# 64 turns of the identity matrix in the opening's waits of TensorE

## The chip, the cores and the metric

The kernel runs on one NeuronCore of a Trainium2 chip. The metric is the device time of one execution in microseconds (us). Three timed runs of the kernel before gave 3094.46, 3094.46 and 3095.07 us, so the median is 3094.46 us.

## The reference, cut to what matters

The program computes two layers of a diffusion backbone on 512 latent tokens and 256 context tokens, 1024 channels wide. Only the start of the first layer matters here:

```python
mod = jnp.split((silu_c @ w_mod[l] + b_mod[l])[:, None, :], 6, axis=-1)
modc = jnp.split(silu_cc @ w_mod[l] + b_mod[l], 6, axis=-1)
u = modulate(rmsnorm(h, g_mix_pre[l]), mod[0], mod[1])      # x * (1 + scale) + shift
uc = modulate(rmsnorm(hc, g_mix_pre[l]), modc[0], modc[1])
y, y_ctx = token_mixers(u, uc, w_in[l], ...)                # begins with u @ w_in
```

The tokens are normalised, then scaled and shifted by vectors that come from two silu'd conditioning vectors times `w_mod`, a matrix that has to be read from memory; then the large product with `w_in` begins. After that come four kinds of token mixers, a gated merge and a feed-forward block, twice.

## The kernel before, in words

Each engine has its own instruction stream, written out by hand and joined by semaphores; nothing is reordered at run time. The weight products are made of three matmuls each (`w_hi`·`u_hi`, `w_hi`·`u_lo`, `w_lo`·`u_hi`): ScalarE (ACT) rounds a landed weight unit to `w_hi` (L1811, in the opening L2132) and VectorE (DVE) makes the rest `w_lo` (L2422, in the opening L2717). `chunk_product` and `half_product` (L1140, L1152) are the two lines where TensorE (PE) multiplies such a unit.

The opening (function `opening(g)` of the tensor block) runs in this order on PE. `turn_tokens(t)` turns each of six token tiles with 8 transposes against `ident` (L1002), two banks of PSUM at a time; ACT and DVE copy them out (L2118, L2702; `x_copied`). `turn_vectors(0)` turns the small vectors. `mod_product(at, half)` (L1030) multiplies the silu'd conditioning vectors by half of the modulation block `at`, four matmuls of 32 columns side by side, each of them two instructions in the trace; it waits for `mod_landed` of its 1 MB load. `first_roots` (L1017) spreads the inverse roots of the norm that GpSimd (POOL, L3381) makes. ACT copies a finished modulation row out (L2097, `row_copied`), `mod_columns(at)` (L1044) turns it into columns of bank 5, DVE adds the bias (L2685, L2691, `pair_made`), and ACT then scales and shifts one channel block k of the tokens (L2103), rounds it to `u_hi` (L2107), and DVE makes `u_lo` (L2697, `first_low`). `first_chunk(g, k)` multiplies that block by the first weight unit: 12 matmuls.

The loads go out from SyncE (SP, queue q1) in program order: the six token tiles, the modulation blocks 0, 4, 1, then the first `w_in` unit, then the blocks 5, 2, 6, 3, 7 (L928, two halves each), the second layer's vectors, two `w_in` units (L852), and 12 small loads that repeat one row to all 128 partitions: `sink`, `gbias` and four of `lam_in` for each layer (L936 to L939). Block `at` of `mod_product` uses load `MOD_LOADS[at]` of (0, 4, 1, 5, 2, 6, 3, 7), so blocks 0 and 1 use loads 0 and 4, block 2 load 1, block 3 load 5. After the opening, SP waits until a 3 MB store of the turned tokens (`h_scratch`, issued by ACT at L2144 after `row(7)`, on queue q10) has landed, and only then issues the loads for the background work: 1 MB blocks of `w_mod` (L835), which DVE multiplies and sums (L2737, L2739) into `part`, and which PE turns in `back_unit` (L1115, four transposes) after waiting for `back_summed`. On DVE this summing stands ahead of the L2422 that makes the next `w_lo`, that of the third weight unit. DVE's first instruction after the opening (L2657) needs all 12 small loads. SP's wait for the store:

```python
                            if phases[index - 1][0] in ("opening", "close"):
                                sp.wait_ge(h_stored, 16 * stored)
```

PSUM banks: the token turns use banks 0 to 3, the vectors bank 4, the modulation columns bank 5, the spread roots 6 and 7, and the first chunks banks 0 to 3. `MOD_BANK` = (0, 1, 4, 6, 7, 4, 6, 7).

Of the kernel before, what the change touches and what calls it, by code (L numbers as in the profile page):

```python
# [27 lines left out]
P = 128  # L28
D_MODEL, SEQ, CTX_LEN, DEPTH, GRID_W, ROPE_BASE = 1024, 512, 256, 2, 64, 10000.0
TOK = CTX_LEN + SEQ  # L30
NT = TOK // P
# [334 lines left out]
def build(nc, x, c, ctx_in, c_ctx, w_mod, b_mod, g_mix_pre, g_mix_post, g_ffn_pre, g_ffn_post, w_in, a_sink,  # L366
# [6 lines left out]
    with stack:  # L373
# [616 lines left out]
        def _(pe):  # L990
# [15 lines left out]
            def turn_vectors(ll):  # L1006

                pe.wait_ge(vectors_in[ll], 16 * 10)
                nc.tensor.transpose(ps[:, 4, 0:N_ROWS], vec_rows[0:N_ROWS, ll, :],
                                    ident[0:N_ROWS, 0:N_ROWS]).then_inc(vec_turned, 1)  # L1010

            def first_roots():

                pe.wait_ge(first_norm, 2)
                for t in range(NT):
                    at = t % 3 * P
                    last = nc.tensor.transpose(ps[:, 6 + t // 3, at:at + P], root[:, t:t + 1].to_broadcast([P, P]),  # L1017
                                               ident[:, :])
                last.then_inc(first_spread, 1)

            def mod_product(at, half):

                if half == 0 and at < 2:
                    pe.wait_ge(x_copied[at], NT - 1)
                if half == 0 and at in (3, 4):
                    pe.wait_ge(x_scaled, KD)
                pe.wait_ge(mod_landed[MOD_LOADS[at]], 16 * 2)
                for c in range(4):
                    k = 4 * half + c
                    last = nc.tensor.matmul(ps[32 * c:32 * c + 32, MOD_BANK[at], 0:256], silu_wide[:, k, :],  # L1030
                                            mod_ring[MOD_LOADS[at]][:, k * 256:(k + 1) * 256], start=half == 0,
                                            stop=half == 1)
                if half == 1:
                    last.then_inc(row_ready, 1)
# [13 lines left out]
            def first_chunk(g, k):  # L1048
# [4 lines left out]
                for j in range(g.nt):  # L1053
                    chunk_product(g, g.u0 % 2, g.t0 + j, j, k)

            def opening(g):

                pe.wait_ge(consts_made, 1)
                for t in range(NT):
                    turn_tokens(t)  # L1060
                    if t == 4:
                        turn_vectors(0)
                pe.wait_ge(scalars_in, 1)
                mod_product(0, 0)
                first_roots()
                mod_product(0, 1)
                mod_product(1, 0)
                mod_columns(0)
                mod_product(1, 1)
                mod_columns(1)  # L1070
                for at in (2, 3):
                    mod_product(at, 0)
                    mod_product(at, 1)
                mod_columns(2)
                mod_columns(3)
                first_chunk(g, 0)
                first_chunk(g, 1)
                for at in (4, 5):
                    mod_product(at, 0)
                    mod_product(at, 1)  # L1080
                first_chunk(g, 2)
                mod_columns(4)
                mod_columns(5)
                for at in (6, 7):
                    mod_product(at, 0)
                    mod_product(at, 1)
                first_chunk(g, 3)
                mod_columns(6)
                mod_columns(7)
                first_chunk(g, 4)  # L1090
                first_chunk(g, 5)
                turn_vectors(1)
                ph.end_products(True)
                first_chunk(g, 6)
                first_chunk(g, 7)
# [2342 lines left out]
```

## Time and profile before

| | us |
|---|---|
| three timed runs | 3094.46, 3094.46, 3095.07 |
| median | 3094.46 |
| the profiled execution | 3094.94 |
| its span, first to last instruction | 3093.2 |
| PE busy | 3018.7 (98% of the span) |
| DVE busy | 1702.3 (55%) |
| ACT busy | 1135.5 (37%) |
| mean granted TensorE clock | 0.995 |

The profiled execution lies 0.48 us above the median; 1.7 us of it lie outside the span. In a timeline a row stands for one instruction or for several equal ones in a row: start, duration of all, engine, line, operation, output and inputs, count, and in brackets how long the engine had been idle and what ended that. The rows of a matmul end later than the next begins, since its tail is counted; the distance of starts is the true pace.

### The profile page before, as it was taken

The page shows a single profiled execution, that of the slowest core. Times are in us where ns is not written, and L with a number is a line of the kernel's source. Part 1 is how long each engine was busy: PE and PEld are TensorE (multiplying, and loading weights), DVE is VectorE, ACT ScalarE, POOL GpSimd, SP SyncE. Part 2 cuts the span into 40 slices and gives each one's busy share as a digit, 9 for nine tenths or more (in the row PEclk, how much of TensorE's full clock was granted, in tenths as well). Part 3 has the DMA queues.
Part 4 walks back from the last instruction along what each step waited for, and adds up shares of the span by engine and source line. Part 5 has one row for each costly group of instructions (what it writes and reads, how often), then busy time and mean ns, then how long its engine had stood idle before and what let it go on. Part 6 is the DMA issues. An engine that isn't in the chain of part 4 may idle for free.

```text
span 3093.2 us, 44400 instructions
## 1 busy us (share of the span) xinstructions
PE 3018.7 (98%) x17548; PEld 2704.4 (87%) x17548; DVE 1702.3 (55%) x3077; ACT 1135.5 (37%) x1919; POOL 187.3 (6%) x153
## 2 busy tenths in 40 slices
PE   8999999999999999999999999999999999999999
PEld 7999978998898899999999997887877977888887
DVE  4844377333367866763362563547444688655334
ACT  5243254333313544222212442435333235532223
POOL 0011000200020000000000000100100210000000
PEclk8999999999999999999999999999999999999999
DMA  8412311310252024531431442241320621543333
GB/s 291 143 34 95 114 42 29 130 62 28 82 170 69 28 96 150 164 115 49 131 109 46 141 130 71 67 138 42 116 75 28 203 68 50 164 136 97 107 89 102
DMA packets 349295, 309.32 MB, mean 100 GB/s; under 512 B 40670, under 2 KB 321196, under 8 KB 347692
## 3 DMA queue, kind: packets, MB, share of 16 engines
q1 hardware_dynamic: 326926, 240.65, 26.1%
q10 hardware_dynamic: 22174, 65.99, 5.9%
q8 instruction: 133, 2.18, 0.3%
q14 instruction: 62, 0.51, 0.1%
HBM read 272.89 MB, written 33.29 MB: 99 GB/s over the span
## 4 chain that ended last, share of the span: by engine, by line
PE 50%; DVE 5%; ACT 1%; issue 1%; DMA 1%; POOL 0%; ACTq 0%; POOLq 0%; DVEq 0%
PE ps L1140 32%; PE ps L1516 5%; PE ps L1152 4%; PE ps L1552 2%; DVE space L2739 1%; PE ps L1594 1%; PE ps L1129 1%; PE ps L1580 1%; PE ps L1546 1%; DVE w_lo L2422 1%; PE ps L1612 1%; DMA space<-in_w_mod 1%; DVE mx L3008 0%; PE ps L1115 0%; PE ps L1766 0%
## 5 line engine op out<-in xcount | busy, mean ns | idle before, releaser
L1140 PE MATMUL ps<-u_hi,w_hi 128*128 128x384 f32 (+1 forms) x1784 | 522.3, 352 | 1.8 <-DVE w_lo L2422 0.7
L1140 PE MATMUL ps<-u_hi,w_lo 128*128 128x384 f32 (+1 forms) x1784 | 517.8, 349 | 0.0
L1140 PE MATMUL ps<-u_lo,w_hi 128*128 128x384 f32 (+1 forms) x1784 | 517.7, 349 | 0.0
L2422 DVE TENSOR_TENSOR w_lo<-w_raw,w_hi 128x2048 fp32r<-128x2048 f32 x129 | 298.3, 2312 | 311.9 <-ACT w_hi L1811 307.9
L1140 PEld LDWEIGHTS ps<-u_hi,w_hi 128*128 128x128 f32 x1784 | 324.3, 188 | 22.2 <-issue 2.7
L1140 PEld LDWEIGHTS ps<-u_hi,w_lo 128*128 128x128 f32 x1784 | 326.3, 188 | 18.6
L1140 PEld LDWEIGHTS ps<-u_lo,w_hi 128*128 128x128 f32 x1784 | 326.3, 188 | 17.9
L1811 ACT ACTIVATE w_hi<-w_raw 128x2048 fp32r<-128x2048 f32 x129 | 246.0, 1907 | 206.2 <-issue 64.6
L1516 PE MATMUL ps<-u_hi,w_hi 128*128 128x384 f32 (+1 forms) x816 | 304.3, 373 | 6.2 <-ACT space L2185 3.5
L1516 PE MATMUL ps<-u_hi,w_lo 128*128 128x384 f32 (+1 forms) x816 | 294.9, 361 | 0.2
L1516 PE MATMUL ps<-u_lo,w_hi 128*128 128x384 f32 (+1 forms) x816 | 293.6, 360 | 0.0
L2739 DVE SCALAR_TENSOR_TENSOR space<-space,silu_c 128x256 f32<-128x256 f32 x560 | 246.7, 482 | 10.1
L3008 DVE TENSOR_REDUCE mx<-ps 128x1 f32<-128x768 f32 (+3 forms) x200 | 156.3, 782 | 115.0 <-PE ps L1552 88.8
L1880 ACT ACTIVATE space<-ps 128x768 f32<-128x768 f32 (+3 forms) x78 | 57.4, 736 | 362.7 <-PE ps L1140 359.0
L1516 PEld LDWEIGHTS ps<-u_hi,w_hi 128*128 128x128 f32 x816 | 154.1, 189 | 23.3 <-ACT space L2185 7.3
L1516 PEld LDWEIGHTS ps<-u_hi,w_lo 128*128 128x128 f32 x816 | 153.8, 189 | 12.1 <-issue 2.1
L1516 PEld LDWEIGHTS ps<-u_lo,w_hi 128*128 128x128 f32 x816 | 154.3, 189 | 10.5 <-issue 1.3
L1850 ACT ACTIVATE hid_hi<-space 128x768 fp32r<-128x768 f32 (+2 forms) x44 | 32.6, 740 | 314.2 <-DVE space L2457 314.2
L2457 DVE TENSOR_TENSOR space<-space,ps 128x768 f32<-128x768 f32 (+1 forms) x44 | 36.1, 821 | 186.2 <-PE ps L1140 180.8
L2201 ACT ACTIVATE space<-ps,nmx 128x768 f32<-128x768 f32 (+3 forms) x160 | 119.4, 747 | 48.2 <-DVE nmx L3014 46.7
L1152 PE MATMUL ps<-u_hi,w_hi 128*128 128x384 f32 (+1 forms) x400 | 128.7, 322 | 5.9 <-DVE w_lo L2422 1.8
L1552 PE MATMUL ps<-space 64*128 64x256 f32 (+2 forms) x784 | 129.3, 447 | 4.9 <-ACT space L2201 4.9
(338 smaller groups left out, 5429.1 us busy)
## 6 DMA issues: line engine op xcount, KB each, us to landing
w_raw<-in_w_in SPq DMA_DIRECT2D x288, 256.0 KB, 3.8
w_raw<-in_w_gate_up SPq DMA_DIRECT2D x176, 256.0 KB, 4.0
space<-in_w_mod SPq DMA_DIRECT2D x40, 1024.0 KB, 5.3
w_raw<-in_w_down SPq DMA_DIRECT2D x114, 192.0 KB, 2.9
w_raw<-in_w_branch SPq DMA_DIRECT2D x64, 256.0 KB, 3.7
w_raw<-in_w_out SPq DMA_DIRECT2D x48, 256.0 KB, 3.7
m_scratch<-space ACTq DMA_DIRECT2D x3, 3072.0 KB, 10.0
space<-in_w_mod SPq DMA_DIRECT2D x16, 512.0 KB, 8.9
```

The lines of the kernel that those rows point to most:

```text
L1140: last = nc.tensor.matmul(ps[:, 2 * (t % 2) + b, 0:a1 - a0], wv[w][:, k, j * P:(j + 1) * P], xx[:, k, a0:a1], start=(k == 0 and w == 0 and ...
L1152: last = nc.tensor.matmul(ps[:, bank, at:at + cols.stop - cols.start], wv[w][:, k, j * P:(j + 1) * P], xx[:, k, cols], start=(k == 0 and w ...
L1516: last = nc.tensor.matmul(ps[:, bank, 0:cols.stop - cols.start], wv[w][:, k, j * P:(j + 1) * P], xx[:, k, cols], start=k == 0 and m == 0, ...
L1552: last = nc.tensor.matmul(ps[:, 2 * slot + at // 512, at % 512:at % 512 + b - a], lhs, rhs(a, b), start=not deep, stop=not here)
L1811: A(w_hi[slot][:, :], w_raw[slot][:, :], ACT.Copy).then_inc(w_hi_done, 1)
L1850: A(hid_hi[:, kk, toks(g.lat)], space[:, 30 + s:31 + s, toks(g.lat)], ACT.Copy).then_inc(hid_hi_done, 1)
L1880: A(tile_at(dst_tile(g, it, s, j), g.lat), acc_of(g, it, s, j, t), ACT.Copy if g.kind == "copy" else ACT.Sigmoid, scale=HD ** -0.5 if g.na ...
L2201: A(p_slot(kind, n.map)[:, 0:w], view, ACT.Exp, bias=nmx[:, n.map % 4:n.map % 4 + 1], scale=c_scale[:, t:t + 1] if kind == "c" else SCALE[ ...
L2422: V.tensor_tensor(w_lo[slot][:, :], w_raw[slot][:, :], w_hi[slot][:, :].bitcast(F32), ALU.subtract).then_inc(w_lo_done, 1)
L2457: V.tensor_tensor(tile_at(30 + s, g.lat), tile_at(30 + s, g.lat), acc(t % 2, g.lat), ALU.mult).then_inc(hid_ready, 1)
L2739: ins = V.scalar_tensor_tensor(part[:, sg], w, silu_c[:, k, sg:sg + 1], part[:, sg], ALU.mult, ALU.add)
L3008: own.did(V.reduce_max(mx[:, c4:c4 + 1], view, AX))
```

## The change

It adds a helper, `idle_turns(count, bank)`, and four calls of it in PE's opening. A turn is `nc.tensor.transpose` of `ident` against `ident` into one of four 128-column places of the named bank. Nothing reads what they write. 8 turns stand after the token turns, 12 between the first half product of block 0 and `first_roots`, 8 before `mod_columns(1)` and 36 between blocks 2 and 3. The last two calls write bank 2, and wait first until ACT has copied all the token turns. Everything else keeps its order.

```diff
+            def idle_turns(count, bank):
+
+                if bank == 2:
+                    pe.wait_ge(x_copied[0], NT)
+                for i in range(count):
+                    at = i % 4 * P
+                    nc.tensor.transpose(ps[:, bank, at:at + P], ident[:, :], ident[:, :])
+
             def opening(g):
 
                 pe.wait_ge(consts_made, 1)
@@
                     turn_tokens(t)
                     if t == 4:
                         turn_vectors(0)
+                idle_turns(8, 5)
                 pe.wait_ge(scalars_in, 1)
                 mod_product(0, 0)
+                idle_turns(12, 5)
                 first_roots()
                 mod_product(0, 1)
                 mod_product(1, 0)
                 mod_columns(0)
                 mod_product(1, 1)
+                idle_turns(8, 2)
                 mod_columns(1)
-                for at in (2, 3):
-                    mod_product(at, 0)
-                    mod_product(at, 1)
+                mod_product(2, 0)
+                mod_product(2, 1)
+                idle_turns(36, 2)
+                mod_product(3, 0)
+                mod_product(3, 1)
                 mod_columns(2)
                 mod_columns(3)
                 first_chunk(g, 0)
```

## Rows read from the trace of the kernel before

**Rows 1.** The page's part 1: busy time and share of the span of each engine.

```profile
PE 3018.7 (98%) x17548; PEld 2704.4 (87%) x17548; DVE 1702.3 (55%) x3077; ACT 1135.5 (37%) x1919; POOL 187.3 (6%) x153
```

**Rows 2.** Timeline of PE, opening: start, duration, line, count, idle before and releaser.

```profile
4.72 4.32 PE L1002 MATMUL ps<-ident,x_tok 128*128 128x128 f32 x24 [4.72 <-DMA x_tok<-in_ctx]
9.31 1.06 PE L1002 MATMUL ps<-ident,x_tok 128*128 128x128 f32 x8 [0.28 <-ACT space L2118]
...
14.92 0.64 PE L1030 MATMUL ps<-space 128*32 128x256 f32 x8 [1.49 <-DMA space<-in_w_mod]
17.41 0.95 PE L1017 MATMUL ps<-ident,root 128*128 128x128 f32 x6 [1.85 <-POOL root L3381]
18.30 1.93 PE L1030 MATMUL ps<-space 128*32 128x256 f32 x16
...
22.78 0.98 PE L1044 MATMUL ps<-picks,space 128*128 128x2 f32 x4 [0.59 <-ACT space L2097]
23.69 1.93 PE L1030 MATMUL ps<-space 128*32 128x256 f32 x16
29.13 1.93 PE L1030 MATMUL ps<-space 128*32 128x256 f32 x16 [3.50 <-DMA space<-in_w_mod]
30.99 1.87 PE L1044 MATMUL ps<-picks,space 128*128 128x2 f32 x8
32.72 0.99 PE L1140 MATMUL ps<-u_hi,w_hi 128*128 128x384 f32 x2
```

**Rows 3.** Stretches: window, length, busy (count) by engine, granted clock, DMA share, GB/s.

```profile
18.00:18.50 0.50, 0.50 (x7) 0.24 (x9) 0.10 (x1) 0.00 (x0) 0.00 (x0) 0.56 1.11 356
...
38.50:39.00 0.50, 0.50 (x5) 0.50 (x4) 0.20 (x1) 0.00 (x0) 0.00 (x0) 0.96 0.91 267
```

**Rows 4.** The same view, of the token turns (L1002) alone: PE, weight loads.

```profile
4.70:7.70 3.00, 2.98 (x14) 3.00 (x15) 1.00 1.03 399
```

**Rows 5.** Timeline of PE, the same kinds of work at full clock.

```profile
39.74 1.93 PE L1030 MATMUL ps<-space 128*32 128x256 f32 x32
41.60 0.61 PE L1140 MATMUL ps<-u_hi,w_hi 128*128 128x384 f32 x2
...
43.81 0.95 PE L1044 MATMUL ps<-picks,space 128*128 128x2 f32 x8
```

**Rows 6.** Timeline of DVE: the low parts of channel blocks 1 and 2.

```profile
33.60 0.96 DVE L2697 TENSOR_TENSOR u_lo<-first_x,u_hi 128x768 fp32r<-128x768 f32 x1 [0.27 <-ACT u_hi L2107]
35.67 0.96 DVE L2697 TENSOR_TENSOR u_lo<-first_x,u_hi 128x768 fp32r<-128x768 f32 x1 [1.11 <-ACT u_hi L2107]
```

**Rows 7.** One line's instructions: the last modulation load, and its issue to landing.

```profile
L928 SPq DMA_DIRECT2D space<-in_w_mod x1: 1888/1888/1888, 31.9 to 31.9; - x1
...
DMA to landing us min/median/max: 9.2/9.2/9.2
```

**Rows 8.** Timelines of ACT's and SP's queues: the 3 MB store, the first background loads.

```profile
46.70 0.37 ACTq L2144 DMA_DIRECT2D h_scratch<-space  x1
...
58.69 1.00 SPq L835 DMA_DIRECT2D space<-in_w_mod  x2
```

**Rows 9.** DMA queues in the stretch 46 to 50: packets, MB, share of 16 engines.

```profile
q1 hardware_dynamic: 898, 0.19, 22.2%
```

**Rows 10.** The same in 51 to 57.

```profile
q10 hardware_dynamic: 99, 2.43, 94.2%
q1 hardware_dynamic: 99, 0.01, 1.1%
```

**Rows 11.** Timelines of DVE and PE, from the background load to the third weight unit.

```profile
64.28 0.17 DVE L2657 TENSOR_SCALAR nsink<-sink 128x16 f32<-128x16 f32 x1 [5.44 <-DMA lam_in<-in_d_lam_k]
...
67.17 0.62 DVE L2737 TENSOR_SCALAR space<-space,silu_c 128x256 f32<-128x256 f32 x2 [1.68 <-DMA space<-in_w_mod]
67.83 6.38 DVE L2739 SCALAR_TENSOR_TENSOR space<-space,silu_c 128x256 f32<-128x256 f32 x14
74.35 2.29 DVE L2422 TENSOR_TENSOR w_lo<-w_raw,w_hi 128x2048 fp32r<-128x2048 f32 x1
...
76.33 0.60 PE L1115 MATMUL ps<-ident,space 128*128 128x128 f32 x4
76.70 0.62 PE L1140 MATMUL ps<-u_hi,w_hi 128*128 128x384 f32 x2
```

**Rows 12.** A later wait and the clock after it: waits of PE, stretches as above.

```profile
PE ps L1219 <- POOL root L3318: 2.3, 1, 2.3
...
1752.00:1755.40 3.40, 3.40 (x12) 3.40 (x11) 3.40 (x5) 0.00 (x0) 0.00 (x0) 0.50 0.42 117
```

## The prediction

> **What bounds the kernel.** I read the page's busy times first: PE is busy for 98% of the span, DVE for 55% [rows 1]. Time is saved only where PE is made to do the same work sooner, and only if nothing later makes it wait for what was saved. The second view is PE's timeline of the opening, the only stretch that the change touches. The reader is to see three idle times there: 1.49 us before 14.92 (modulation load 0), 1.85 us before 17.41 (POOL's roots) and 3.50 us before 29.13 (load 5) [rows 2]. The third view is the granted clock by stretches: full up to 18.0, 0.56 on average in 18.0 to 18.5, so it fell to the lower level (1.2 GHz) near 18.06, and it came back to 2.4 GHz near 38.54 [rows 3]. PE had been idle for most of the time from 15.5 to 17.4 before the fall. So PE worked 20.5 us of the opening at half clock. The turns can only pay by keeping the clock up there; they compute nothing.
>
> **What a turn costs.** At full clock 8 token turns start to finish in 1.06 us, with a tail of 0.27 for the last: about 0.11 us a turn [rows 2]. At half clock 14 turns began in 3.00 us: 0.21 us a turn [rows 4]. That stretch is also printed with clock 1.00, but its pace says that the clock was low until about 7.7 us: 24 turns took 4.32 us, not 2.8 [rows 2, 4]. No matmul of another kind had run by then. So turns by themselves raised the clock here, and I take it that they can hold it. The Trainium skill, "TensorE: Matmul & The Clock Gate", Part 4, says the opposite: in transpose mode the clock gate does not open, since it does not count as PE being busy in the same way. By that sentence the 64 turns would only be extra work at half clock. The trace disagrees, as the pace of the first 24 turns shows.
>
> **The change part by part.** (1) 8 turns after the token turns: 0.9 us from 13.4, inside the 1.49 us wait: nothing. (2) 12 turns after 15.5: 1.3 us, over by 16.9, while the roots come at 17.41: nothing, and 0.5 us of idle time is left of 1.85. I take the clock as held here. (3) 8 turns before `mod_columns(1)`: the work from 18.30 to 22.2 took half-clock paces; at full clock 32 product instructions take 1.86 us (39.74 to 41.60) and 8 of `mod_columns` 0.88, half of 1.86 for 16 and 1.73 for 8 at low clock [rows 2, 5]. So block 1 ends at about 20.2 and the 8 turns run to 21.1, over ACT's row copy that PE waited 0.59 us for before. Then `mod_columns(1)` and block 2 follow, to about 22.6. Their wait for `x_copied` has been met since 16. (4) 36 turns from 22.6: 36 x 0.11 = 3.9 us, to 26.6. Load 5 still lands at 29.1, as no load in q1 waits for PE in this stretch. So 2.5 us of idle time stay. They are hidden by the load; behind them the queue is as before.
>
> From 29.13 on, the terms of the gain. Block 3: 16 instructions, 1.86 to 0.93. `mod_columns(2)` and `(3)`: 1.73 to 0.88 plus 0.15 for the row copy, so chunk 0 starts at 31.1, not 32.72. Its 12 matmuls take 2.2 us at full clock (41.60 to 43.81) [rows 5], so it ends at 33.3. Chunk 1 needs the low part of block 1, whose chain (row copy, ACT, DVE) moves by 0.93 only: 33.60 + 0.96 becomes 33.65 [rows 6]. PE waits 0.4 there, runs chunk 1 to 35.9 and begins block 4 at 36.0 instead of 39.74. **The opening gains 3.7 us.** The next bounds: block 2's low part at 35.7 is ready before PE's 37.9 [rows 6]; the last modulation load lands at 31.9 + 9.2 = 41.1 [rows 7] and is wanted at 41.9. So 3.7 us stand until the opening ends.
>
> **Where the gain goes.** The point that decides is 76.70, where PE starts its third weight unit. DVE ends the `w_lo` for it at 74.35 + 2.29 = 76.64, and PE comes from its four turns at 76.33 + 4 x 0.11 = 76.77 [rows 11]. The slack is nil: to keep 3.7 us, that `w_lo` must come 3.7 us earlier. It stands on DVE behind the background sums, and these waited for a `w_mod` load until 67.17; in between DVE does 9.5 us of work without a gap [rows 11]. Does that landing move? The 3 MB store is issued at 46.70 when `row(7)` is out [rows 8], so it moves to 42.96, and its first packets from about 49.9 to about 46.2. While the store runs, q1 gets one packet for each of the store's: 99 and 99 in 6 us, against 898 in the 4 us before it [rows 9, 10]. These 898 are mostly the small repeated loads. Started 3.7 us earlier, the store pushes in front of 3.7 us of them (some 840 packets), of which about 60 slip through during it. They have to be moved after it, in the 3.7 us that the store was early. Behind them in q1 stand the last `lam_in` loads, and behind those the `w_mod` load. So the store ends 3.7 us earlier and q1's rest has, at the 225 packets a us of rows 9, 780 / 225 = 3.5 us more to do: the landing moves by -0.3 us by that count. I take 0, since other loads share the engines behind the store, and let it go 0.6 to either side. The farthest bound is -3.7, the load moving with its issue.
>
> The Trainium skill, "DMA: Bandwidth & Descriptors", Queues, rings and completion order, says that an engine takes turns between queues by whole packets of some 9 to 17 descriptors. If that held for what the rows count, q1 would send 9 or more small ones for each of the store's, all of the 840 would pass during the store, and the 3.7 us would be kept. The trace shows one for one [rows 10], so I give that less weight.
>
> So PE arrives at 72.6, finds `back_summed` missing until 74.2, does its four turns, and then waits for `w_lo` until 76.7: 3.7 us of idle time in two pieces. **The gain is gone**, and the clock is in danger again. A wait of 2.3 us near 1749 to 1751 was followed by a stretch of 3.4 us at half clock [rows 12], and there are three such places late in the trace. In such a stretch PE does half: 1.7 us lost. The sum: -3.7 + 3.7 + 1.7 = +1.7 us. On the profiled execution's own 3094.94 that is 3096.6; it lies 0.48 above the median of the runs, so 3096.2 us. The later 3000 us only shift: PE is the bound there, and what it waits for hangs on its own products.
>
> **The rivals.**
> - *Given back at 76.7, as above*: 3096.2, from 3093.9 (the landing 0.6 earlier, no fall of the clock) to 3098.5 (0.6 later, two stretches of half clock). For it: no slack at 76.70 and one packet for one. Against: the small loads may run faster behind the store. Chance 0.46.
> - *The clock falls all the same* in the 2.5 us between 26.6 and 29.1. The late wait of 2.3 us had it fall [rows 12], 1.49 us before 14.92 had not. Then block 3 and chunks 0 and 1 run at half clock as before, the store doesn't move, and the time is that of before: 3094.5, 1 us to either side. Chance 0.29.
> - *The gain is kept*, if the landing moves with the store: 3094.46 - 3.74 = 3090.7. For it: SP issues the `w_mod` load at 58.69, right after the store lands, and the store moves. Against: the queue in front of the load [rows 9 to 11]. Chance 0.19.
> - *Slower: turns don't hold the clock.* It falls at 18.06. The 8 turns cost 8 x 0.21 - 0.59 = 1.1, so block 2 ends at 26.7; 36 x 0.214 = 7.7 us take PE to 34.4, where load 5 was there at 29.1: 5.3 us late, with all behind it, 3099.8. It decides from the point where 36 turns outlast the load, 29.1. If the long run of turns lifts the clock midway, as the first 24 did, most of that comes back. This is the result of the page's sentence on transposes above. Chance 0.04.
> - The rest, 0.02: three late dips of the clock may fall elsewhere once everything is shifted, each worth up to 1.7 us; this also widens each case.
>
> **How the numbers follow.** The likeliest case gives 3096.2 us. Low 3090.3 takes in the kept gain, high 3098.6 the two stretches of half clock. 0.2% is 6.2 us, about what a measurement of this kernel can tell from no change: faster needs 3088.3 or less, which only the kept gain with two late dips gone could reach (0.04); slower needs 3100.6, the fourth case and a little more (0.03); the same 0.93.
>
> **What would show it.** The step of the clock: 1.00 from 18 to 31. The cost of the turns: `mod_product` of block 3 still at 29.1. The gain: chunk 0 at 31.1, the product of block 4 at 36.0, the store issued at 43.0. The loss: DVE's L2737 still at 67.2, an idle wait of PE at L1115 near 72.6 to 74.2, L1140 again at 76.7, and a clock of 0.5 for some us after. If L2737 starts at 63.5, the third case holds; if the clock reads 0.5 at 30, the second; if block 3 starts after 30, the fourth.

## The result, and the profile after

| | before | after |
|---|---|---|
| median of 15 timed runs each, us | 3095.07 | 3099.85 |
| ratio after to before | | 1.0015, 95% interval 1.0009 to 1.0022 |
| profiled execution | 3094.94 | 3097.78 |
| its span | 3093.2 | 3096.0 |
| mean granted TensorE clock | 0.995 | 0.997 |

The changed kernel is slower by 4.7 us in these runs (by their means; one run of each kernel, of 3729 and 6049 us, lies far above its others and is left out of means and ratios). It lies within 0.2% of the kernel before, as forecast, but above the forecast range (3090.3 to 3098.6, against 3096.2). Two more measurements of the same kernel, on other chips, gave less, 1.7 and 3.9 us (below); over all 36 runs of the three sets, each set against the kernel before beside it, it is 3.5 us slower. The lines behind the insert have moved by 13: L1115 is now L1128, L1140 L1153, L2422 L2435, L2737 L2750. The turns are L1062.

First the page's part 1 of the changed kernel, against [rows 1]: PE has 64 instructions more, and nothing else changes its work.

```profile
PE 3022.0 (98%) x17612; PEld 2709.8 (88%) x17612; DVE 1701.6 (55%) x3077; ACT 1135.0 (37%) x1919; POOL 189.0 (6%) x153
```

PE's timeline of the changed kernel, the stretch of [rows 2, 5, 11]; in brackets the idle time before and what ended it:

```profile
13.37 1.04 PE L1062 MATMUL ps<-ident 128*128 128x128 f32 x8
14.44 0.64 PE L1030 MATMUL ps<-space 128*32 128x256 f32 x8
15.01 1.53 PE L1062 MATMUL ps<-ident 128*128 128x128 f32 x12
17.52 0.87 PE L1017 MATMUL ps<-ident,root 128*128 128x128 f32 x6 [0.98 <-POOL root L3394]
...
20.63 1.09 PE L1062 MATMUL ps<-ident 128*128 128x128 f32 x8
21.99 1.07 PE L1030 MATMUL ps<-space 128*32 128x256 f32 x16
23.00 4.15 PE L1062 MATMUL ps<-ident 128*128 128x128 f32 x36
28.59 1.07 PE L1030 MATMUL ps<-space 128*32 128x256 f32 x16 [1.45 <-DMA space<-in_w_mod]
29.59 1.19 PE L1044 MATMUL ps<-picks,space 128*128 128x2 f32 x8
30.64 0.60 PE L1153 MATMUL ps<-u_hi,w_hi 128*128 128x384 f32 x2
...
35.53 1.93 PE L1030 MATMUL ps<-space 128*32 128x256 f32 x32
...
73.11 0.66 PE L1128 MATMUL ps<-ident,space 128*128 128x128 f32 x4 [0.81 <-DVEq L2768]
75.48 0.62 PE L1153 MATMUL ps<-u_hi,w_hi 128*128 128x384 f32 x2 [1.72 <-DVE w_lo L2435]
```

The reader is to see the opening's gain and its loss. The product of block 4 begins at 35.53, where it began at 39.74: 4.2 us gained. The third weight unit begins at 75.48, where it began at 76.70: 1.2 us are left, since PE waits before and after its four turns, for the background sum and then for `w_lo`.

DVE's timeline of the changed kernel shows the release of both waits, against [rows 11]:

```profile
62.98 0.17 DVE L2670 TENSOR_SCALAR nsink<-sink 128x16 f32<-128x16 f32 x1 [8.35 <-DMA lam_in<-in_d_lam_k]
...
65.95 0.62 DVE L2750 TENSOR_SCALAR space<-space,silu_c 128x256 f32<-128x256 f32 x2 [1.76 <-DMA space<-in_w_mod]
...
73.13 2.29 DVE L2435 TENSOR_TENSOR w_lo<-w_raw,w_hi 128x2048 fp32r<-128x2048 f32 x1
```

The store behind which this load is issued went out 4.2 us earlier, at 42.48 instead of 46.70 [rows 8] (ACT's queue of the changed kernel); the first sum came only 1.2 us earlier, at 65.95 instead of 67.17.

```profile
42.48 0.39 ACTq L2157 DMA_DIRECT2D h_scratch<-space  x1
```

The view by stretches of the changed kernel (window, length, busy with count of PE, weight loads, DVE, ACT and POOL, granted clock, DMA share, GB/s):

```profile
28.00:31.00 3.00, 2.41 (x26) 1.85 (x27) 1.73 (x4) 1.98 (x5) 0.00 (x0) 1.00 1.09 348
76.40:79.80 3.40, 3.40 (x13) 3.40 (x12) 3.26 (x9) 0.00 (x0) 0.00 (x0) 0.50 1.07 378
```

The clock stayed at its upper level through the whole opening, where it had been at the lower one from 18.06 to 38.54 [rows 3], and fell to the lower level (1.2 GHz) for 3.4 us right behind the wait for `w_lo`. The time from the third unit to one later matmul, at 94.58 before and 94.97 after, was 17.88 us before and 19.49 after: 1.6 us for that stretch. So at 94 us the sum is -1.2 + 1.6 = +0.4 us. From there to one matmul near 3000 the execution took 2907.9 us instead of 2905.5. **Most of the 2.8 us between the two profiled executions arises in the part of which the forecast said that it only shifts.**

Something does change there. DVE's first background sum of the second layer, before:

```profile
2439.81 0.62 DVE L2737 TENSOR_SCALAR space<-space,silu_c 128x256 f32<-128x256 f32 x2 [5.24 <-DMA space<-in_w_mod]
```

and in the changed kernel, where it waits 1.3 us longer for its load:

```profile
2441.72 0.62 DVE L2750 TENSOR_SCALAR space<-space,silu_c 128x256 f32<-128x256 f32 x2 [6.53 <-DMA space<-in_w_mod]
```

The DMA queues of the changed kernel in 2428 to 2442 (packets, MB, share of 16 engines), while that load is under way:

```profile
q10 hardware_dynamic: 1328, 2.62, 56.4%
q1 hardware_dynamic: 1855, 1.88, 40.2%
q8 instruction: 1, 0.02, 0.4%
```

The same view of the kernel before has no load of instructions in it. It has 242 packets more of q1, in part because the load went out 0.6 us earlier there (2428.22, not 2428.83):

```profile
q10 hardware_dynamic: 1328, 2.62, 56.2%
q1 hardware_dynamic: 2097, 2.12, 45.6%
```

PE's waits between 2470 and 2525 in the changed kernel (total, times, longest):

```profile
PE ps L1128 <- DVEq L2768: 3.9, 1, 3.9
...
PE ps L1128 <- DVE mod_t L2774: 0.4, 1, 0.4
```

Before, the first of these was 3.3 us (L1115) and the second was not there.

### The profile page after: what moved, and what is told of

It reads as the page before. It is cut to its first block, busy times and chain, and to the rows that moved or that the text cites. A ratio compares the mean times of both kernels' runs of the same rounds, so it can differ in the third digit from the quotient of the medians.

```text
span 3096.0 us, 44528 instructions
## 1 busy us (share of the span) xinstructions
PE 3022.0 (98%) x17612; PEld 2709.8 (88%) x17612; DVE 1701.6 (55%) x3077; ACT 1135.0 (37%) x1919; POOL 189.0 (6%) x153
## 4 chain that ended last, share of the span: by engine, by line
PE 51%; DVE 5%; ACT 1%; issue 1%; DMA 1%; POOL 0%; ACTq 0%; POOLq 0%; DVEq 0%
PE ps L1153 32%; PE ps L1529 6%; PE ps L1165 4%; PE ps L1565 2%; DVE space L2752 1%; PE ps L1607 1%; PE ps L1142 1%; PE ps L1593 1%; PE ps L1559 1%; DVE w_lo L2435 1%; PE ps L1625 1%; DMA space<-in_w_mod 1%; DVE mx L3021 0%; PE ps L1128 0%; PE ps L1779 0%
## 5 line engine op out<-in xcount | busy, mean ns | idle before, releaser
L1153 PE MATMUL ps<-u_hi,w_hi 128*128 128x384 f32 (+1 forms) x1784 | 521.9, 352 | 3.9 <-DVE w_lo L2435 2.5
L1153 PE MATMUL ps<-u_hi,w_lo 128*128 128x384 f32 (+1 forms) x1784 | 517.5, 349 | 0.0
L1153 PE MATMUL ps<-u_lo,w_hi 128*128 128x384 f32 (+1 forms) x1784 | 517.3, 349 | 0.0
L2435 DVE TENSOR_TENSOR w_lo<-w_raw,w_hi 128x2048 fp32r<-128x2048 f32 x129 | 297.4, 2305 | 313.0 <-ACT w_hi L1824 308.9
L1153 PEld LDWEIGHTS ps<-u_hi,w_hi 128*128 128x128 f32 x1784 | 323.7, 188 | 24.9 <-DVE w_lo L2435 3.3
L1153 PEld LDWEIGHTS ps<-u_hi,w_lo 128*128 128x128 f32 x1784 | 326.0, 188 | 18.4
L1153 PEld LDWEIGHTS ps<-u_lo,w_hi 128*128 128x128 f32 x1784 | 326.1, 188 | 18.0
L1529 PEld LDWEIGHTS ps<-u_hi,w_lo 128*128 128x128 f32 x816 | 154.1, 189 | 12.1 <-issue 2.1
```

Of the source, the lines that this page charges most:

```text
L1153: last = nc.tensor.matmul(ps[:, 2 * (t % 2) + b, 0:a1 - a0], wv[w][:, k, j * P:(j + 1) * P], xx[:, k, a0:a1], start=(k == 0 and w == 0 and ...
L1529: last = nc.tensor.matmul(ps[:, bank, 0:cols.stop - cols.start], wv[w][:, k, j * P:(j + 1) * P], xx[:, k, cols], start=k == 0 and m == 0, ...
L2435: V.tensor_tensor(w_lo[slot][:, :], w_raw[slot][:, :], w_hi[slot][:, :].bitcast(F32), ALU.subtract).then_inc(w_lo_done, 1)
```

## The experiments

**Theories.** Q, the forecast's: the background load is held by the 12 small loads ahead of it in q1, so the opening's gain waits at the third unit, and half clock follows. C, its rival: the clock falls in the gap before load 5 all the same. I, formed only after the result: the changed length of PE's program shifts the loads of instructions and so costs time near 2440. "Run beside" means timed against the kernel before on the same chip. The sets ran on different chips, so only kernels of one set, or the ratios, are compared. An interval of 0.0009 to either side is 2.8 us.

In the table, each kernel's profiled execution: the start of the product of load 5, of block 4, of the third weight unit, of the matmul near 94, the way from there to near 3000, and the stretches of half clock between 8 and 94 (start/length; in the two kernels with waits added they are counted from 15). The last columns are the ratio to the kernel before, run beside, with its interval.

| kernel | load 5 | block 4 | unit 3 | 94 | 94 to 3000 | half clock | ratio | 95% |
|---|---|---|---|---|---|---|---|---|
| before | 29.13 | 39.74 | 76.70 | 94.58 | 2905.5 | 18.1/20.5 | | |
| before_again | 27.73 | 38.38 | 75.30 | 93.16 | 2905.5 | 16.7/20.5 | 1.0001 | 0.9992 to 1.0010 |
| after | 28.59 | 35.53 | 75.48 | 94.97 | 2907.9 | 76.4/3.4 | 1.0015 | 1.0009 to 1.0022 |
| after_again | 28.65 | 36.62 | 74.91 | 92.80 | 2907.0 | 31.0/3.4 | 1.0004 | 0.9995 to 1.0013 |
| after_third | 28.80 | 35.74 | 76.57 | 96.03 | 2908.5 | 76.9/3.4 | 1.0012 | 1.0003 to 1.0021 |
| e_late | 29.57 | 39.05 | 76.02 | 93.88 | 2909.1 | 31.0/6.8 | 0.9997 | 0.9988 to 1.0006 |
| e_late_b | 29.00 | 39.23 | 76.19 | 94.05 | 2908.2 | 17.1/3.4, 27.3/10.2 | 0.9995 | 0.9986 to 1.0004 |
| e_split | 29.68 | 37.65 | 75.70 | 93.58 | 2907.1 | 31.6/3.4 | 1.0000 | 0.9991 to 1.0009 |
| e_split_b | 27.61 | 37.93 | 75.53 | 93.42 | 2907.6 | 22.7/13.7 | 0.9996 | 0.9987 to 1.0005 |
| e_no36 | 29.11 | 38.82 | 77.84 | 95.75 | 2905.9 | 26.3/10.2 | 0.9999 | 0.9990 to 1.0008 |
| e_hold | 28.66 | 35.57 | 75.04 | 92.90 | 2907.3 | none | 1.0004 | 0.9995 to 1.0013 |
| e_60 | 29.86 | 36.81 | 75.58 | 93.50 | 2906.4 | none | 1.0001 | 0.9992 to 1.0010 |
| e_60_hold | 29.60 | 36.55 | 75.99 | 93.85 | 2906.3 | none | 1.0006 | 0.9997 to 1.0015 |
| e_late60 | 29.74 | 36.67 | 73.64 | 91.50 | 2905.6 | none | 0.9987 | 0.9978 to 0.9996 |
| late60_again | 29.73 | 36.67 | 73.62 | 91.48 | 2906.8 | none | 0.9988 | 0.9979 to 0.9997 |
| e_pad | 32.83 | 40.82 | 78.16 | 96.01 | 2906.4 | 35.0/3.4 | 1.0003 | 0.9994 to 1.0012 |
| e_pad_b | 35.16 | 44.45 | 81.39 | 99.26 | 2909.9 | 21.2/20.5 | 1.0022 | 1.0013 to 1.0031 |

**The kernels once more: after_again, after_third, before_again.** No edit.

> The changed kernel once more, for a second profile and a second set of times. The clock's steps fell at different places in the profiles so far, so one profile shows one draw of them. Theory Q with the clock: PE waits about 3 us near 72 to 76 again, a stretch of 3.4 or 6.8 us at half clock follows, and the median is 4 to 5 us over the kernel before. Rival (the first set was slow by chance): within 1 us of the kernel before.

> The changed kernel for the third time, since its two sets of times differ by more than their spread (4.7 and 1.7 us over the kernel before, each by about 0.8). If both draw from one spread, this set lies between them: 2 to 5 us over. Its profile is a third draw of where the clock falls.

> The kernel before once more, for a second profile of it. One profile can't say whether its 20.5 us of half clock in the opening are usual. The two e_*_b profiles had 13.7 us. If that is usual, chunk 0's product of block 4 comes 1 to 2 us sooner than 39.74 here too, and the turns have less to gain than 3.7 us. Time within 1 us of the kernel before.

Measured: medians of 3097.5 and 3099.38 us for the changed kernel, against 3095.64 and 3095.02 of the kernel before beside it; 3095.05 for the kernel before. The second set missed its expectation of 4 to 5 us, the third met its own. The second profile of the changed kernel shows rival C in small. Stretches of after_again:

```profile
31.00:34.40 3.40, 3.40 (x12) 3.40 (x11) 1.29 (x5) 3.34 (x6) 0.00 (x0) 0.50 1.09 347
```

The clock fell there behind the 1.5 us wait for load 5, block 4 came 1.1 us later than in the first profile, and at 76 it did not fall. After_third is like the first profile, with a longer wait at PE's four turns, as its first sum came at 67.05:

```profile
74.19 0.66 PE L1128 MATMUL ps<-ident,space 128*128 128x128 f32 x4 [1.69 <-DVEq L2768]
```

So the same program steps its clock at other places from one execution to the next, and the first sum is at 65.95, 65.39 and 67.05 in three executions of it, at 67.17 and 65.70 in two of the kernel before. One profile is one draw. On average over these the first sum moved by 66.13 - 66.44 = -0.3 us, and the matmul near 94 by 94.6 - 93.9 = +0.7.

**The small loads moved: e_late and e_late_b.** The 12 small loads are issued after the fourth weight unit, behind the first background loads, and DVE's part that needs them (`scalars`) moves to where it is first used. In e_late_b the same edit is made in the kernel before.

```diff
-            for ll in range(DEPTH):
-                sp.dma_start(sink[:, ll, :], a_sink[ll:ll + 1, :].partition_broadcast(P)).then_inc(bcast_in, 16)
...
                         if not isinstance(it, int) or g.u0 + s + 2 * it >= 3:
                             load_unit(g, it, s)
+                        if isinstance(it, int) and g.u0 + s + 2 * it == 3:
+                            small_loads()
...
-                if g.name == "misc" and g.layer == 0:
-                    scalars()
...
                 if unit == 1:
+                    if l == 0:
+                        scalars()
```

> The changed kernel, with the 12 small repeated loads issued by SP after the fourth weight unit instead of before the 3 MB store, and DVE's work on them (L2670 to L2675) moved to the place where it first needs them. Theory Q (the small loads stand in q1 in front of the first w_mod load, and the store pushes them back): that load lands before 61, DVE's first background sums start by then, PE shows no wait at L1128 or for the third unit near 72, no half clock near 76, and the 4.2 us of the opening are kept: 3090.5 us or less, some 4 to 5 us under the kernel before. Rival B (the w_mod load is late by the bandwidth of the engines, whatever stands in front of it): sums still start near 65 to 66, and the time stays near 3099.

> The kernel before with the same move of the small loads and nothing else. Theory Q: PE had no wait near 76 before, so it gains nothing there: 3095 us, within 1 us of the kernel before. Rival (the move helps by itself, for example since PE was held up by less than its tails show): a gain of 1 us or more without any turns.

DVE's first sum in e_late:

```profile
62.07 0.61 DVE L2754 TENSOR_SCALAR space<-space,silu_c 128x256 f32<-128x256 f32 x2 [3.92 <-DMA space<-in_w_mod]
```

It starts at 62.07 instead of 65.95, and PE doesn't wait at the third unit at all. So the small loads did hold the background load: that part of theory Q holds. The time missed its expectation of 3090.5 us or less: it is 3094.44 against 3094.84, no gain over the kernel before. In the profiled execution the opening had hardly a gain to keep (block 4 at 39.05); but that execution took 3097.89 us, 3.5 above the median of the set, and does not tell what the others did. PE of e_late at load 5, and the stretch behind it:

```profile
29.57 1.07 PE L1034 MATMUL ps<-space 128*32 128x256 f32 x16 [2.34 <-DMA space<-in_w_mod]
...
31.10:37.80 6.70, 6.70 (x23) 6.65 (x23) 2.79 (x6) 6.09 (x9) 0.00 (x0) 0.50 1.09 348
```

Load 5 landed a microsecond later, the wait before it was 2.34 us, and 6.8 us at half clock followed: rival C. The kernel e_late_b (3095.06 us) had no gain to keep, and none showed, as expected.

**The store in halves: e_split and e_split_b.** Two stores of half the columns, so that the store's packets are of 1.5 KB and not 24 KB and q1 gets its turn oftener; e_split_b is the same in the kernel before.

```diff
-                stored += {"opening": 1, "close": 2}.get(phase[0], 0)
+                stored += {"opening": 2, "close": 2}.get(phase[0], 0)
...
-                act.dma_start(h_dram[:, :, :], space[:, 8:16, :]).then_inc(h_stored, 16)
-                n.h_out += 1
+                for c in (slice(0, WT // 2), slice(WT // 2, WT)):
+                    act.dma_start(h_dram[:, :, c], space[:, 8:16, c]).then_inc(h_stored, 16)
+                    n.h_out += 1
```

> The changed kernel, with the 3 MB store issued as two halves of the token columns, so that its packets have 1.5 KB and not 24 KB. Theory Q (q1 gets one packet for each packet of the store, so large packets starve the small loads): q1 moves several hundred packets while the store runs, the first w_mod load lands near 62 to 63, PE's wait near 72 to 75 shrinks to under 0.5 us and the time is near 3091 to 3092. Rival B: the landing stays near 66 and the time near 3099; it may be worse, as smaller packets take longer.

> The kernel before with the same split store and nothing else. Theory Q: the small loads had passed before the store but for the last five, so the first w_mod load lands 0 to 4 us earlier, without a use for it on PE: 3095 us, within 1 us of the kernel before. Rival B: up to 2 us slower, since the store takes longer and holds up the loads behind it.

In e_split the small loads did get through earlier. Its DMA queues in 47 to 53, and its DVE:

```profile
q10 hardware_dynamic: 1010, 1.54, 68.5%
q1 hardware_dynamic: 732, 0.12, 10.7%
```

```profile
59.18 0.17 DVE L2671 TENSOR_SCALAR nsink<-sink 128x16 f32<-128x16 f32 x1 [2.43 <-DMA lam_in<-in_d_lam_k]
...
66.18 0.61 DVE L2751 TENSOR_SCALAR space<-space,silu_c 128x256 f32<-128x256 f32 x2 [5.79 <-DMA space<-in_w_mod]
```

The last small load had landed by 59.18 instead of 62.98, and yet the first sum came at 66.18. A miss, whose reason stands in SP's queue and its landing times. The background load of e_split, issued at 60.74, was there 5.4 us later:

```profile
60.74 1.01 SPq L835 DMA_DIRECT2D space<-in_w_mod  x2
...
DMA to landing us min/median/max: 5.4/6.7/8.0
```

That of the changed kernel, issued at 56.45, took 9.5 us. Here it is with the last two small loads ahead of it on SP:

```profile
51.32 4.32 SPq L939 DMA_DIRECT2D lam_in<-in_d_lam_q  x1
55.68 0.65 SPq L939 DMA_DIRECT2D lam_in<-in_d_lam_k  x1
56.45 1.03 SPq L835 DMA_DIRECT2D space<-in_w_mod  x2
...
DMA to landing us min/median/max: 9.5/10.7/12.0
```

The halves let 732 small packets through in 6 us instead of about 130, so the queue ahead of the load was empty, worth 4.1 us. But the store landed near 60.7 instead of 54.6, and SP issued the load 4.3 us later. Of these 6.1 us, 4.0 are the price of the halves (16.1 us from issue to landing, not 12.1); the other 2.1 come from this execution's smaller gain in the opening, where the store went out at 44.60 and not 42.48. Had it gone out at 42.48, with everything behind it shifted alike, the first sum would have come near 64.1, an estimate: 1.9 us earlier than in the changed kernel. The times are 3095.49 us (e_split, where 3091 to 3092 was expected) and 3094.41 us (e_split_b, as expected) against 3094.84.

The two small loads above show a second hold. In the changed kernel's first profile the store had landed at 54.59, but SP was still issuing small loads, one of them for 4.32 us, until 56.33. So there the background load was issued 1.9 us after the store's landing, where SP waited for the store in the kernel before (landed 58.60, issued 58.69). In the other two profiles of the changed kernel it was issued 0.1 us after the store. In e_late60 (below) the small loads stand behind the background load, and both halves of the gain are there: issued at 55.72, landed 5.3 us later.

**The 36 turns left out: e_no36.**

```diff
-                idle_turns(36, 2)
```

> The changed kernel without its 36 turns; the 28 others stay. Theory Q: PE is idle for 5 us before load 5, the clock falls there and chunks 0 and 1 run at half clock, so the opening gains 0 to 2 us only, the store isn't much earlier, and PE's wait near 75 is shorter by the same: 3094 to 3096, 3 to 5 us under the changed kernel. Rival (the turns of the other three places do the harm, for example at the roots): it stays near 3099.

PE at load 5, and the stretch behind:

```profile
29.11 1.93 PE L1030 MATMUL ps<-space 128*32 128x256 f32 x16 [6.00 <-DMA space<-in_w_mod]
...
26.40:36.40 10.00, 7.29 (x36) 6.11 (x37) 5.26 (x7) 7.73 (x14) 0.00 (x0) 0.50 1.09 348
```

The other 28 turns held the clock from 18 to 26; in the 6 us wait it fell and took block 3 and chunk 0 back to the old pace. Block 4 began at 38.82, 3.3 us behind the changed kernel. So nearly all of the opening's gain hangs on the 36. In this execution the first sum came late, at 68.32, and the third unit at 77.84 behind 1.72 us of waiting for `w_lo`; the clock held behind that wait. The time, 3095.45 against 3095.64, is in the expected 3094 to 3096, but 2.1 us under the changed kernel of the same set and not 3 to 5.

**60 turns instead of 36: e_60 and, with the clock held at the third unit, e_hold and e_60_hold.** 60 turns fill PE up to load 5. The hold adds 7 turns before the first `back_unit` and 16 behind it, for the two waits at the third unit; e_hold has it with 36 turns, e_60_hold with 60.

```diff
-                idle_turns(36, 2)
+                idle_turns(60, 2)
```

```diff
-                if bank == 2:
+                if bank in (2, 7):
...
+                            held = isinstance(it, int) and bk.b0 + i == 0
+                            if held:
+                                idle_turns(7, 7)
                             back_unit(bk, i)
+                            if held:
+                                idle_turns(16, 6)
```

> The changed kernel with 60 turns instead of 36, so that they last until load 5, and the small loads left where they are. Theory Q: the clock is always held in the opening, so PE always waits about 3 us near 72 to 76, and mostly loses the clock there: 3098 to 3100, no faster than the changed kernel, though more of the opening is at full clock. Beside e_late60 (3091.93) it shows what the small loads in front of the w_mod load cost: 6 to 8 us. Rival (the 36 turns are too few, and that alone is the fault): 3092.

> The changed kernel with 23 more turns where PE waits for the background sums and the third weight unit: 7 before the first back_unit, into bank 7, and 16 after it, into bank 6. Nothing else is moved, so the wait for DVE stays. If the fall of the clock behind that wait costs 1.7 to 3.4 us, as its length of 3.4 or 6.8 us says, this kernel is 1.7 to 3.4 us faster than the changed one: about 3096 to 3098, and its clock reads 1.00 from 76 to 83. Rival (the loss is in the wait alone): no difference, 3099.

> e_60 with the 23 turns of e_hold at the wait near 72 to 76. If the clock's fall behind that wait costs 1.7 to 3.4 us, this is that much faster than e_60: 3095 to 3097. If the wait alone is the loss, it equals e_60.

In e_60 the wait for `w_lo` is there as in the changed kernel, 1.58 us up to 75.58. Its 60 turns outlast the landing of load 5: block 4 begins at 36.81, 1.3 us behind the changed kernel. In e_hold the turns fill it, and the clock is full behind it:

```profile
72.17 0.93 PE L1062 MATMUL ps<-ident 128*128 128x128 f32 x7
...
73.38 1.91 PE L1062 MATMUL ps<-ident 128*128 128x128 f32 x16
...
75.00:80.00 5.00, 5.00 (x32) 5.00 (x31) 4.79 (x13) 0.00 (x1) 0.00 (x0) 1.00 0.96 343
```

Unit 3 to the matmul near 94 takes 17.9 us where the clock held (17.86 in e_hold, 17.89 in after_again) and 19.5 where it fell (19.49 and 19.46): 1.6 us, with the 17.88 of the kernel before from five profiles of the same work. But the fall behind `w_lo` is no certain one: e_60 waited 1.58 us and e_no36 1.72, as long as the changed kernel, and the clock held. The times don't separate these kernels (1.0004, 1.0001 and 1.0006, intervals of 0.0009 to either side), and each has another length of PE's program, so their differences are not put down to the turns. Against its expectation e_60 missed: 3095.67 us, not 3098 to 3100. The medians of e_hold (3096.40) and e_60_hold (3096.05) lie where they were expected, but e_60_hold is no faster than e_60, so the 1.6 us rest on the profiles alone.

**Both causes taken away: e_late60 and late60_again.** The edit of e_late together with 60 turns instead of 36; the second is the same kernel once more.

> The changed kernel with the small loads and DVE's work on them moved as in e_late, and 60 turns instead of 36, so that they last until load 5 lands. In the profile of e_late PE was idle for 2.5 us between the turns and load 5 and the clock fell at 31.1, so its opening kept little. Theory Q with the clock: now the clock stays up through the opening and PE doesn't wait near 72 to 76: 4 us under the kernel before, near 3091. Rival (something else near the end of the opening gives the gain back): 3094 to 3095 as e_late.

> e_late60 once more: the turns lengthened to 60, the small loads behind the fourth weight unit. If its gain is real, it is again 3 to 4.5 us under the kernel before, near 3091.5, and its PE shows no wait near 72 to 76.

PE and DVE of e_late60:

```profile
23.04 6.77 PE L1066 MATMUL ps<-ident 128*128 128x128 f32 x60
29.74 1.07 PE L1034 MATMUL ps<-space 128*32 128x256 f32 x16
...
73.28 0.60 PE L1132 MATMUL ps<-ident,space 128*128 128x128 f32 x4
73.64 0.60 PE L1157 MATMUL ps<-u_hi,w_hi 128*128 128x384 f32 x2
```

```profile
61.05 0.62 DVE L2754 TENSOR_SCALAR space<-space,silu_c 128x256 f32<-128x256 f32 x2 [5.28 <-DMA space<-in_w_mod]
```

No bracket is left on PE: it waits neither for load 5 nor at the third unit, and no stretch of half clock lies between 8 and 94 in either profile. The third unit begins at 73.64, 3.1 us before that of the kernel before, whose second profile had 75.30. The time is 3091.93 us against 3095.64, and 3091.95 against 3095.7 in the repeat: **3.7 us faster than before, twice, with intervals that end below 1**. This is the version that beats the kernel before, and in its set it is 5.6 us under the changed kernel (3097.5). Against e_60, whose turns are the same, only the small loads differ: the opening is alike (block 4 at 36.81 and 36.67), the first sum comes at 61.05 and not 66.06, and the third unit at 73.64 and not 75.58. That pair shows what holds the opening's gain back. The pair of e_late and e_late60 is less clean, for the 24 more turns also take away the longer wait near 2440 (the last pair of kernels below). Of its gain the profiles place 2.4 us in the first 94 us (91.5 against 93.9, the mean of the two of before); the rest they don't place, and two profiles on either side can't.

**The length of PE's program: e_pad_b and e_pad.** Waits on a semaphore that is long met lengthen PE's program by about 8 KB in e_pad_b (from before) and by 8 KB more than the change's own in e_pad (from after). The expectation of e_pad_b, put on record before it ran, gives the 64 turns the same 8 KB; no trace shows the size of a program.

```diff
-                pe.wait_ge(consts_made, 1)
+                for _ in range(145):
+                    pe.wait_ge(consts_made, 1)
...
+                    for _ in range(112 if at == 3 else 0):
+                        pe.wait_ge(consts_made, 1)
```

This is e_pad_b; in e_pad the second group is 56 waits before block 3 and 56 behind the first `back_unit`.

> The kernel before with 257 waits on a semaphore that is long set, in two places where PE is idle (its start and the wait for load 5). They make PE's program 8 KB longer, exactly as much as the 64 turns do, and compute nothing. Theory I (the length of the program decides where a 16 KB load of instructions falls): the q8 packet falls between 2430 and 2440, the background sums of the second layer start 41.3 to 41.6 us after the matmul near 2400, and the time is 1 to 2 us over the kernel before. Rival (the turns or the shift of the opening did it): sums after 39.9 to 40.1, time as the kernel before.

> The changed kernel with 257 such waits, in three idle places, so that its program is 16 KB longer than that of before and not 8 KB. Theory I: the load of instructions falls outside of that stretch again, sums after 39.9 to 40.1, and the time is 1 to 2 us under the changed kernel: 1 to 2.5 us over the kernel before. Rival: sums after 41.3 or more, 3 to 4 us over the kernel before.

DVE's second-layer sum in e_pad_b:

```profile
2448.10 0.62 DVE L2740 TENSOR_SCALAR space<-space,silu_c 128x256 f32<-128x256 f32 x2 [6.53 <-DMA space<-in_w_mod]
```

and in e_pad:

```profile
2442.66 0.62 DVE L2756 TENSOR_SCALAR space<-space,silu_c 128x256 f32<-128x256 f32 x2 [5.22 <-DMA space<-in_w_mod]
```

The kernel before gets the longer wait with 8 KB added and no turn in it; the changed kernel loses it with 8 KB more. That settles theory I for this wait. Over all kernels, it is 6.5 to 6.6 us in the six profiles whose program is 8 KB longer (the three of after, e_late, e_split, e_pad_b) and 5.2 to 5.3 in the eleven others. In each of the six a load of instructions of 16 KB (queue q8) starts 5.9 to 6.2 us before the sum, while the background load is under way. In ten of the eleven none starts between that load's issue and its landing. In e_no36 one does, 0.1 us before the first half lands, and there the second half comes 4.5 us behind the first and not 3.0.

PE's wait for the background unit near 2518 splits the kernels in the same way: 3.9 us in the six, 3.2 to 3.3 in the eleven. From a matmul near 2400 to the end of that wait the six took 1.3 to 1.7 us longer than the kernel before, and the eleven 0 to 0.4.

The time of e_pad_b missed its expectation: 3103.21 us, 7.5 over the kernel before where 1 to 2 were expected, since the added waits were not free; e_pad's, 1.9 over, lies within its 1 to 2.5. For that reason neither time prices the longer program. PE's first turns in e_pad_b:

```profile
10.29 6.56 PE L1002 MATMUL ps<-ident,x_tok 128*128 128x128 f32 x40 [10.29 <-issue]
```

## Why the prediction was wrong, and where it was right

**The price of a turn: right.** 36 turns took 3.9 us (from 23.00 to 27.15, less the tail of 0.27), as forecast. The wait left before load 5 was 1.45 us, not 2.5, since the turns began 0.4 us late and the load came 0.5 us early. **Turns hold the clock: right**, in all three profiles from 18 to the wait for load 5, where the kernel before had been at half clock. What e_no36 adds: without the last 36 it falls in the wait. This goes against the Trainium skill, "TensorE: Matmul & The Clock Gate", Part 4, which says that the clock gate does not open in transpose mode; here turns alone held the upper level, and in e_late60 did so over 6.8 us without any other matmul. The trace calls a turn a MATMUL; whether it runs in the mode that the page means, it does not tell.

**The opening's gain: right in place, near in size.** 4.2 us in the first profile (35.53 against 36.0 forecast), 3.1 and 4.0 in the others against the same 39.74. But 39.74 was itself one draw; the second profile of before had 38.38, and by the averages of three and two the gain is 3.1 us, not 3.7.

**Rival C was not a rival but a share of the executions.** The forecast gave the fall of the clock before load 5 a chance of 0.29 and 3094.5 us. It fell there in one of three profiles of the changed kernel, with 1.1 us lost (3.4 us of half clock), not the whole gain; in e_late it took 6.8 us of half clock. The error was to treat it as one or the other for all runs.

**Given back at the third unit: right.** The forecast had the background load unmoved, -0.3 by its count; the averages of three and two profiles differ by -0.3. That the numbers agree is luck: single executions of one kernel differ by up to 1.7 us there. The third unit itself began at 75.65 on average, against 76.00 before: 0.3 us were left of the opening's 3.1. The two waits are there (0.8 and 1.7 us in the first profile), and e_late60 beside e_60 shows the cause, the small loads in q1. In number it was not so simple: the load was issued 2.2 us earlier (56.45 against 58.69 [rows 8]) and took the longer to land, and in that profile SP's own issuing of the small loads held it for 1.9 us, which the forecast did not have. And rival 3's condition, small loads that pass during the store, would have kept only part of the gain: in e_split they pass, and the store takes 4.0 us longer. The forecast's packet for packet stands, as the DMA view of the changed kernel in 46 to 52 shows:

```profile
q10 hardware_dynamic: 103, 2.53, 98.6%
q1 hardware_dynamic: 130, 0.02, 1.9%
```

1.3 small packets for each of the store's 24 KB ones, not nine or more. The Trainium skill, "DMA: Bandwidth & Descriptors", Queues, rings and completion order, has an engine drain a packet of some 9 to 17 descriptors before it switches; what this view counts as packets alternated nearly one for one.

**The clock behind the wait: right in size, not in chance.** 1.6 us measured, 1.7 forecast, but in two of three profiles, and not in e_60 and e_no36 behind waits of like length.

**The step that failed: "The later 3000 us only shift."** The forecast's sum ended at the third unit with +1.7 us. There and up to 94 it was about right or even high: +0.4 in the first profile, +0.7 by the averages of three and two. Behind 94 the three profiles of the changed kernel took 2907.8 us on average, the two of before 2905.5: +2.3 us that the sum did not have, since it put this whole stretch at nothing. Of these, about 1.5 arise at two places: 0.8 to 1.0 near 2481, where PE waits for the late background sum, and 0.7 at the wait near 2518 (3.9 against 3.3). Both mark the six profiles whose program is 8 KB longer, e_pad_b with no turn in it among them (0.6 to 1.0 and 0.7); in the eleven others, e_pad among them, they are 0 to 0.3 and 0. So their cause is the length of PE's program, which puts a load of instructions among the transfers near 2440; how the second wait follows from it is not shown. The rest, about 0.7 us, arises behind 2518, where these executions have 3.4 us more of half clock, at 2633 in the first and next to the stretch near 2518 in the others. Whether that hangs on the change stays open: all six have it, but six of the eleven others have it too.

By the averages, +0.7 and +2.3 make +3.0, near the +3.5 of the 36 runs. Why the 15 runs of the first measurement lay 4.7 above and those of another 1.7 stays open; the three sets ran on different chips, the places at which the clock steps differ between executions, and so do some waits. PE waited 1.2 us near 2283 in the first profile of the changed kernel, 0.6 and 0.5 in the other two, and 0 and 0.5 in the two of before:

```profile
2283.41 0.62 PE L1153 MATMUL ps<-ckv_hi,w_hi 128*128 128x384 f32 x2 [1.16 <-DVE space L2497]
```

**Two errors of the range.** It was centred on the median of three runs, 3094.46, where 15 gave 3095.07; and it took in the clock's stretches only as cases, each worth 1.7 us, not as a spread that any execution has. The high end would have needed 1.3 us more.

## What to carry to other kernels

Filling waits with idle turns pays only if the engine keeps no other wait behind: here neither the longer fill (e_60) nor the moved loads alone (e_late) gave a gain over the kernel before that could be measured, and both together gave 3.7 us. Part of the step from e_late to the two together may be the longer wait near 2440, which e_late has and they do not; no run separates that. When an engine comes earlier, follow the next load that it needs back through its queue and look at what small transfers stand ahead of it. And count added instructions as bytes: here they moved the loads of instructions, and a transfer 2400 us later was late for it.

## What the runs showed of the hardware

- 8 KB more of PE's program made one background load 1.3 us later near 2440, and 16 KB more did not: the wait was 5.2 to 5.3 us with no addition, with less (e_no36) and with more, and 6.5 to 6.6 at 8 KB, in 17 profiles without exception.
- Waits that hold nothing back cost time in number: with 145 of them ahead of its first turn, PE began its token turns at 10.29 us, not 4.72 [rows 2]. Whether the waits themselves take it or the loading of their instructions, no run separates.
- A store of 24 KB packets starved small ones: 103 of its packets went out beside 130 small ones in 6 us, and SP took 4.32 us from 51.32 on to issue one of the small loads.
- The clock's steps are not fixed by the program. Three executions of one program fell at 76.4, 31.0 and 76.9 us; the length of the wait doesn't tell alone. After 1.52 us of waiting for load 5 it fell (after_again), after 1.45 and 1.75 us at the same place it didn't (after, after_third).
